# A planned attention order, four turn banks, and attention output kept transposed, in a one-layer encoder step

## The reference

```
z = rms(x, g_pre_mix) @ w_in        -> q, k, v (8 heads x 64), forget logits, B, C, u
attention: softmax_s(q_t.k_s / 8 + sum_{s<j<=t} log sigmoid(f_j + b_f)) @ v,  s <= t
conv:      B * causal_conv3(C * u)                       (512 channels)
mix = concat(rms(attn, g_attn_out), rms(conv, g_conv_out)) @ w_o
x   = x + rms(mix, g_post_mix)
x   = x + rms(relu(rms(x, g_pre_mlp) @ w_up)^2 @ w_down, g_post_mlp)
```

## Time and profile before

| | |
|---|---|
| median of 3 runs | 2739.94 us (2737.48 to 2744.5) |
| profiled execution | 2737.44 us, its span 2735.8 us |
| TensorE busy | 2664.9 us (97%), 14966 instructions |
| VectorE, ScalarE, GpSimd busy | 1515.6, 1126.6, 1300.7 us |
| DMA | 364.26 MB, mean 133 GB/s |
| granted TensorE clock | 9 tenths or more in all 40 slices of the span |

### The profile page before, as it was taken

One profiled execution on the slowest core, in us unless ns is written; L12 is line 12 of the kernel. 1 busy time (PEld: TensorE's weight loads), 2 busy tenths in 40 slices (PEclk: granted clock), 3 DMA queues, 4 the chain that ended last, 5 costly groups with the idle time before them and its releaser, 6 DMA issues.

```text
span 2735.8 us, 41595 instructions
## 1 busy us (share of the span) xinstructions
PE 2664.9 (97%) x14966; PEld 2405.3 (88%) x14966; DVE 1515.6 (55%) x2603; ACT 1126.6 (41%) x2099; POOL 1300.7 (48%) x884
## 2 busy tenths in 40 slices
PE   8999999998999999999999999899999999999997
PEld 8999999897888888888889989889999988999996
DVE  5233344247888887765344344665556564556554
ACT  3201301107777877555333332534333344333433
POOL 3233334220101006553477776766556677566654
PEclk9999999999999999999999999999999999999999
DMA  6643534574565443568444546421211272212213
GB/s 199 199 123 110 175 108 142 189 199 103 124 150 122 100 102 117 167 183 244 143 168 163 196 169 225 170 74 64 77 61 61 85 277 96 73 61 66 72 61 108
DMA packets 294353, 364.26 MB, mean 133 GB/s; under 512 B 37576, under 2 KB 245392, under 8 KB 290128
## 3 DMA queue, kind: packets, MB, share of 16 engines
q1 hardware_dynamic: 257152, 316.15, 37.7%
q0 software_dynamic: 11808, 26.74, 3.1%
q10 hardware_dynamic: 25264, 19.66, 2.1%
HBM read 264.30 MB, written 97.94 MB: 132 GB/s over the span
## 4 chain that ended last, share of the span: by engine, by line
PE 46%; DVE 2%; POOL 1%; DMA 1%; issue 1%; ACT 0%; SPq 0%; DVEq 0%; POOLq 0%; ACTq 0%
PE dn_bank L3006 17%; PE up_bank L2982 15%; PE dn_bank L2962 7%; PE up_bank L2937 7%; DMA m_raw_up<-in_w_up 1%; DVE m_raw_up L2758 1%; POOL m_y L2517 1%; POOL m_w_up L2466 1%; DVE m_t L2758 0%; SPq L2342 0%; ACT m_junk L2659 0%; DVE m_y L2863 0%; DMA m_x<-scratch_x 0%; POOL m_u L2509 0%; DVE m_y L2817 0%
## 5 line engine op out<-in xcount | busy, mean ns | idle before, releaser
L3006 PE MATMUL dn_bank<-m_w_dn,m_u 128*128 128x512 f32 x2304 | 531.0, 391 | 5.4 <-ACT m_y L2692 4.3
L3006 PEld LDWEIGHTS dn_bank<-m_w_dn,m_u 128*128 128x128 f32 x2304 | 432.7, 188 | 96.0 <-ACT m_y L2692 4.0
L2982 PE MATMUL up_bank<-m_h,m_w_up 128*128 128x384 f32 x2688 | 476.1, 337 | 8.7 <-DVE m_stage L2772 4.5
L2982 PEld LDWEIGHTS up_bank<-m_h,m_w_up 128*128 128x128 f32 x2688 | 470.1, 189 | 12.7 <-issue 5.1
L2819 DVE TENSOR_TENSOR m_y<-dn_bank,m_y 128x1024 f32<-128x1024 f32 x168 | 205.7, 1224 | 270.4 <-PE dn_bank L3006 270.4
L508 POOL TENSOR_TENSOR w_lo<-w_raw,w_hi 128x1024 fp32r<-128x1024 f32 x72 | 176.0, 2448 | 342.3 <-DVE w_hi L722 342.3
L2509 POOL TENSOR_TENSOR m_u<-m_stage,m_u 128x384 fp32r<-128x384 f32 x128 | 141.5, 1128 | 281.7 <-ACT m_u L2648 281.7
L2466 POOL TENSOR_TENSOR m_w_up<-m_raw_up,m_w_up 128x512 fp32r<-128x512 f32 x128 | 192.2, 1521 | 65.2 <-ACT m_w_up L2616 65.2
L938 PE MATMUL proj<-ha_hi,w_hi 128*128 128x384 f32 (+1 forms) x640 | 212.1, 331 | 0.0
L1446 DVE TENSOR_TENSOR p_lo<-t_bank,p_hi 128x512 fp32r<-128x512 f32 (+1 forms) x336 | 197.9, 599 | 25.2 <-ACT p_hi L1393 24.6
L938 PE MATMUL proj<-ha_hi,w_lo 128*128 128x384 f32 (+1 forms) x640 | 210.0, 328 | 0.0
(11 more groups left out here) (304 smaller groups left out, 5674.4 us busy)
## 6 DMA issues: line engine op xcount, KB each, us to landing
m_raw_up<-in_w_up SPq DMA_DIRECT2D x48, 1024.0 KB, 5.4
m_raw_dn<-in_w_down SPq DMA_DIRECT2D x47, 1024.0 KB, 4.9
w_raw<-in_w_in SPq DMA_DIRECT2D x72, 512.0 KB, 4.1
scratch_h_pairs<-m_pieces POOLq DMA_DIRECT2D x12, 1792.0 KB, 8.2
m_h<-scratch_h_pairs SPq DMA_DIRECT2D x14, 1536.0 KB, 10.8
nck<-scratch_ncum SPq DMA_DIRECT2D x8, 1312.0 KB, 19.2
scratch_v_hl<-vhl SPq DMA_DIRECT2D x20, 512.0 KB, 2.7
q_hi<-scratch_q_hi SPq DMA_DIRECT2D x16, 528.0 KB, 7.3
```

The costliest lines, as they stand in the source:

```text
L2982: mm = pe.matmul(out, w_up[:, j, wp, k, :], hidden_rows(g, j, hp, k), start=(k == 0 and p == 0), stop=(k == KH - 1 and p == 2))
L3006: mm = pe.matmul(bank[:, cols], part, wd[:, wp, b, cols], start=(b == 0 and p == 0), stop=(b == 1 and p == len(passes) - 1))
```

## The change

Attention's output stays transposed, and the N steps go. ScalarE copies the two halves of o_bank to two tiles of 64 partitions (L1445, L1446), GpSimd adds them and multiplies by scales, a row of reciprocals broadcast over 64 partitions; SyncE stores to attn_t. The reciprocals come to that row by DRAM: VectorE turns them in 32-column blocks (rtotal_t), SyncE stores the blocks (L1315) to scratch_rtotal and loads the row back broadcast (L1322). o_t has two places (A_BUFS = 2), and ScalarE waits for the store of the group before the last. There are four t_bank; n_bank is gone. All heads are unrolled into one list, in the group order 0, extra, 1, 2, 3, and attention_order plans each engine's queue by simulated times with fixed costs.

SyncE loads a later head in three parts, at its groups 0 (queries, keys), extra (decay) and 1 (values). w_o is split early: from group number 5 on, each third group a piece of w_o is loaded, scaled by the gains g_attn_out and g_conv_out, split by GpSimd and stored to scratch; GpSimd's own queue loads the whole in head 7. Mixing takes both halves transposed: the turn and the row scaling go, the squares of both halves are made on GpSimd and summed by two small products (L1973 was one).

```diff
-S_BANKS, T_BANKS, O_BANKS = 3, 3, 1
-A_BUFS = 5
+S_BANKS, T_BANKS, O_BANKS = 3, 4, 1
+A_BUFS = 2
+GROUP_ORDER = (0, EXTRA, 1, 2, 3)
+W_FIRST, W_EVERY = 5, 3
+FIRST_CHOICE = {"pe": "VTS", "dve": "TS", "act": "OTM"}
...
+            def store_scales(q):
+                line = dr["rtotal"][q.head:q.head + 1, q.rows]
+                pieces = line.rearrange("o (c b r) -> (o b) c r", c=q.n, r=32)
+                sp.wait_ge(recip_done, q.k + 1)
+                for b in range(wide(q) // (32 * q.n)):
+                    sp.dma_start(pieces[b], rtotal_t[32 * b:32 * b + q.n, q.k % 2, :]).then_inc(rtotal_stored, 16)
...
+            def load_scales(q):
+                sp.wait_ge(rtotal_stored, 16 * q.stores)
+                if q.k >= 2:
+                    sp.wait_ge(att_done, q.k - 1)
+                line = dr["rtotal"][q.head:q.head + 1, q.rows]
+                sp.dma_start(scales[0:HD, q.k % 2, 0:wide(q)], line.to_broadcast([HD, wide(q)])).then_inc(scales_loaded[q.k % 2], 16)
...
+            def fetch(head, at):
+
+                par = head % 2
+                if head >= 2 and at == 0:
+                    sp.wait_ge(used, P_BUFS + groups[GROUPS_OF * (head - 1) - 1].products[-1].at + 1)
...
+            for q in groups:
+                if q.head < HEADS - 1:
+                    fetch(q.head + 1, q.k % GROUPS_OF)
...
+                store_scales(q)
+                load_scales(q)
+                k, at = divmod(q.k - W_FIRST, W_EVERY)
+                if 0 <= k < KB and at == 0:
+                    load_piece(k)
+                if 0 <= k < KB and at == 2:
+                    store_piece(k)
+                if q.k:
+                    store(groups[q.k - 1])
...
-                    act.wait_ge(in_rows, upto("O", it, x.at) + 1)
-                    act.activation(o_t[:, x.at % 2, 0:width], o_bank[x.at % O_BANKS][:, 0:width], ACT.Copy).then_inc(o_taken, 1)
...
+                    act.wait_ge(used, P_BUFS + q.products[-1].at + 1)
+                    if q.k >= A_BUFS:
+                        act.wait_ge(att_stored[q.k % A_BUFS], 16 * (q.k // A_BUFS))
+                    bank = o_bank[q.k % O_BANKS]
+                    act.activation(o_t[0:HD, q.k % A_BUFS, 0, 0:q.wide], bank[0:HD, 0:q.wide], ACT.Copy)
+                    act.activation(o_t[0:HD, q.k % A_BUFS, 1, 0:q.wide], bank[HD:P, 0:q.wide], ACT.Copy).then_inc(o_taken, 1)
...
+                    if x.first:
+                        dve.wait_ge(exp_done, q.maxima[-1].at + 1)
+                        dve.reciprocal(rtotal[:, q.k % 2, 0:q.n], total[:, sums(q)]).then_inc(recip_made, 1)
+                        if q.k >= 2:
+                            dve.wait_ge(rtotal_stored, 16 * groups[q.k - 2].stores)
+                        dve.wait_ge(recip_made, q.k + 1)
+                        dve.transpose(rtotal_t[:, q.k % 2, :], rtotal[:, q.k % 2, :]).then_inc(recip_done, 1)
...
-            def turn(t, s):
-                pe.wait_ge(S["ag_done"], t + 1)
-                if not isinstance(t, int) or t >= 1:
-                    pe.wait_ge(S["a_lo_done"], t)
-                for j in range(CJ):
-                    tr = pe.transpose(t_bank[:, j * P:(j + 1) * P], ag[:, j * P:(j + 1) * P], ident[:, :])
-                tr.then_inc(S["a_turned"], 1)
```

More of the change, by code:

```diff
@@ new lines, with __init__ @@
+EXTRA = QT // 4
+GROUP_ORDER = (0, EXTRA, 1, 2, 3)
+W_FIRST, W_EVERY = 5, 3
+FIRST_CHOICE = {"pe": "VTS", "dve": "TS", "act": "OTM"}
+class Group:
+    def __init__(self, k, head, g):
+        self.k, self.head, self.g, self.par = k, head, g, head % 2
+        self.extra = g == EXTRA
+        self.tiles = [QT] if self.extra else list(range(4 * g, 4 * g + 4))
+        self.n = len(self.tiles)
+        self.rows = slice(SEQ, ROWS) if self.extra else slice(4 * g * P, 4 * g * P + 4 * P)
+        self.wide = P if self.extra else 512
+        self.set = 0 if self.extra else g % 2
+        self.before = None
+        self.stores = 0
+        self.scores, self.maxima, self.turns, self.products, self.out = [], [], [], [], None
@@ new lines, in store, with stored, load_piece @@
+            def store(q):
+                sp.wait_ge(att_done, q.k + 1)
+                sp.dma_start(dr["attn_t"][q.head * HD:(q.head + 1) * HD, q.rows], o_t[0:HD, q.k % A_BUFS, 0, 0:wide(q)]).then_inc(att_stored[q.k % A_BUFS], 16)
+            def stored(q):
+                sp.wait_ge(att_stored[q.k % A_BUFS], 16 * (q.k // A_BUFS + 1))
+            def load_piece(k):
+                sp.wait_ge(w_split, 2 * k)
+                sp.wait_ge(w_stored, 32 * k)
+                sp.dma_start(w_piece[:, :].bitcast(F32), front.piece("w_o", k)).then_inc(w_loaded, 16)
@@ L1335, in _ @@
+            sp.wait_ge(used, P_BUFS + final[2].products[-1].at + 1)
+            front.load_rows(sp)
+            store(groups[-1])
+            for q in groups[-A_BUFS:]:
+                stored(q)
         @block.gpsimd
         def _(pool):
-            pool.sem_inc(added, 1)
             pool.memset(q_hi[1][:, ROWS:].bitcast(F32), 0.0)
@@ L1524, in attend @@
-        return last
+            for x in queues["pe"]:
+                step(x)
+        return {
+            "scores_free": lambda pe: pe.wait_ge(taken, S_BANKS + ALL_TAKEN),
+            "turns_free": lambda pe: pe.wait_ge(lo_done, T_BANKS + ALL_TURNED),
+            "outputs_free": lambda pe: pe.wait_ge(o_taken, O_BANKS + len(groups)),
+        }
 AXIS_BYTES = 2 * RT * P * 4 + (ROWS + PAST) * 4
```

754 lines of the change are left out of this document (325 added, 429 removed).

## The result

The changed kernel took **2856.3 us** (median of 4 runs, 2855.41 to 2858.39) beside 2738.78 us for the kernel before in the same session (2737.48 to 2744.5): a ratio of 1.0426, 95% interval 1.0408 to 1.0444. The forecast was 2808 us, the range ended at 2852. The direction was right, the size was not: 117.5 us were lost where 68 were forecast, and the time lies 4 us above the range.

The account below looks back on a forecast made before the run. TensorE was taken as the bound, busy 97% of the span, with any stop in attention paid in full. From 2737.4 us, gains of 32 and losses of 100 gave 2805, forecast 2808 us with the median's offset; range 2786 to 2834, stretched 2750 to 2852.

Parts of the forecast that it names:

- The wait, its place and its size: Attention, ScalarE's output copy of the extra group: waits for a store, 14 us (10 to 16), 13 us lost each, heads 1 to 6.
- t0: End of a head's last value product in attention, where ScalarE copies it out; the forecast counts landings from it.
- the 5 us of head 0: Attention, head 0: the store of group 0 lands near 654 us, its user comes at 649.80 less 1, costing 5 us.
- Losses ... = 100 us: Attention: 78 for the waits, 14 for w_o pieces, 3 in head 3, 5 in head 0; between 65 and 130 us.
- I count 1 us as won back: Attention: during each 14 us wait TensorE issues turns and scores it needed anyway, so 13 us are lost.
- The granted clock is 1.00 in both, the 2.4 GHz level, and I expect it to stay: Attention and mixing: TensorE's clock keeps its full level after the change.
- So a small transfer waits for the bytes ahead of it: SyncE's queue: totals behind six loads (3.5 MB, 16 us) land after 17 to 20.6 us, the store after 20 to 25.
- Half the wait: Rival, attention: small stores land sooner, 7 us lost for 13 and half the pieces' cost; 2761 us, chance 0.16.
- faster: Rival, attention: the store is already there when ScalarE reaches the copy, only gains count; 2708 us, chance 0.12.
- VectorE becomes the bound besides: Rival, attention: totals' work and a wait for their store add 10 us idle, waits of 16 us; 2841 us, chance 0.10.
- The order: TensorE in attention: planner regroups the same work, 106 fewer changes of kind give 9.5 us; idle time falls 5 us.
- Mixing 5 us shorter: Mixing, TensorE: four transposes per tile go, one sum-of-squares product comes, 17 x 0.29 = 5 us gained.

## Why the prediction was off

**The wait, its place and its size: right.** "ScalarE's copy of a group's output (L1445) now waits until the store of the group before the last has landed": its line has 101.6 us where some 90 were forecast, longest 17.6 for 13 to 20. The store landed at t0 + 24.8 for 20 to 25. Six waits of 14.3 to 17.6 us stand in heads 1 to 6; in head 3 a further 2.7 us for the 3 forecast; the 5 us of head 0 didn't come, and 1.7 us came late in the last head. The natural place of the copy was t0 + 7.5, not + 9, which alone makes the waits 1.5 us longer each.

**"Losses ... = 100 us": 112 us.** Taking both waits out gave 111.9 us. The price per us of waiting was a little above one, not below it: "I count 1 us as won back" stands against a restart at half clock, by an estimate from the rows at 792.90 to 796.92 some 4 us of work at half speed, about 2 us each. "The granted clock is 1.00 in both, the 2.4 GHz level, and I expect it to stay" was wrong: 0.90 on average in attention.

**"So a small transfer waits for the bytes ahead of it": right on the landing, short on the reason.** In the changed kernel the totals do land behind the loads ahead of them, at t0 + 18.8. But the runs with stores or loads on another queue show small transfers landing after 11 to 15 us too, with the 16 DMA engines full, so order on one queue is not what it takes. The row that carried the argument was also misread. Of the 21.4 us of the 32 KB load 18.93 were SyncE's issue of it; it landed 2.4 us behind the end of that issue:

```profile
749.13 18.93 SPq L102 DMA_DIRECT2D v_hl<-scratch_v_hl  x1
```

The forecast of the landing came out because it didn't rest on the reason: 3.5 MB at 217 GB/s keep the engines full for 16 us under either. Half the wait (2761 us) didn't come, and neither did faster (2708 us): in each of heads 1 to 6 ScalarE waited over 14 us for the store.

**The totals' wait was named, and only in a rival.** "VectorE becomes the bound besides" gave it 10 us of idle time. It was 62.2 us, 57.6 of them under the other wait, so it cost the changed kernel nothing and cost 65.6 us once the first wait alone was undone.

**"The order": the step that failed.** 27 of the 32 us of gain were to come in attention (14 for the transposes, 9.5 for changes of kind, 5 of idle time, less 1.5 at the border); the runs show 1.4. The transposes were removed from TensorE, but its queue then met VectorE, with 36.0 us of waits at the score banks. A change of kind still has its price in the row (0.32 us for 0.23, 796.92 to 797.24 in the changed kernel), but it did not decide: the order with most of them was the fastest. The step that misled is that TensorE's time was taken as a sum of its own work, with VectorE at 381 of 462 us beside it; how VectorE's work is spread over the new order wasn't looked at.

**Mixing 5 us shorter, and an MLP untouched: true without the shift.** With the gains on top, mixing took 218.7 us, 3.7 less than before. The 32-byte shift, 18.8 us with four outputs and 19.3 in the kernel before, was put at nothing: it was in no term and no rival.

By the runs, then: +111.9 for the waits, +18.8 for the shift, and -5.9 for all else (2725.56 against 2731.47) make 124.8 us over a kernel before of 2731.5, that is 2856.3. Forecast were +100, 0 and -32, on a base of 2739.9. The misses of 11.9, 18.8 and 26.1 us, less 8.4 us of base (2739.9 to 2731.5, which later runs of the kernel before show and no part of the change explains), are the 48.3 us between 2808.0 and 2856.3; of these the order's is the largest, and with any one of the three terms right the time would have been inside the range.

## What to carry to other kernels

When a change cuts the number of places for something that leaves by DMA, look at what fills the DMA engines at that moment. Here stores of 128 KB and of half a kilobyte took 11 to 15 us beside the loads whatever their queue, and moving them shortened attention by 18 us at most (574 to 556); more places in flight removed the wait, and half-used partitions could hold them. When a wait is removed and little comes back, look for a second wait under it: here the first alone gave 46 us, the second alone nothing, both 112, and the waits' table of the first trace already showed both. And before crediting a removed instruction, check in the new order whether the engine beside it can follow: eight pairs in a row on TensorE are eight steps in a row on VectorE, 0.61 us each for 0.46.

## What the runs showed of the hardware

32 bytes of unused memory per partition ahead of the tiles made the same kernel 0.81% slower (0.64 to 0.99), with 512-column products of 395 instead of 389 ns in mixing and MLP. 3216 products (408 in mixing, 2808 in the MLP) took 6 ns more each, which makes 19 us by estimate. The 392 products from m_w_dn_even take 394 ns in the kernel before as well. Shifts of 64 and 128 bytes slowed them as well (394 and 393 ns in mixing), and putting the tiles of these stages back where they stood restored 389. Which tile matters, and why, stays open: no run moved one tile alone. The fourth turn bank wasn't tested by itself either.
